# Sixteen of the 22 inner chunks of two down projections as seven block products instead of eight

## The reference, cut to what matters

```python
def _swiglu(x, w_gu, w_down):
    gate, up = jnp.split(x @ w_gu, 2, axis=-1)
    return (jax.nn.silu(gate) * up) @ w_down
...
h = _layernorm(ALPHA * x + 0.5 * _swiglu(x, p['ffa_w_gu'], p['ffa_w_down']), p['ln1_g'], p['ln1_b'])
...
y = _layernorm(ALPHA * h + 0.5 * _swiglu(h, p['ffb_w_gu'], p['ffb_w_down']), p['ln3_g'], p['ln3_b'])
```

## Time and profile before

| | |
|---|---|
| median of three runs | 1212.16 us (1209.61 to 1213.62) |
| span of the profiled execution | 1212.0 us |
| TensorE busy | 1180.2 us in 12282 matmuls |
| VectorE busy | 819.3 us |
| ScalarE busy | 512.3 us |
| GpSimd busy | 90.4 us |
| FFN a | from about 8 to 373 us of the span |
| FFN b | from about 861 us to the end |

### The profile page before, as it was taken

One profiled execution on the slowest core, in us unless ns is written; L12 is line 12 of the kernel. 1 busy time (PEld: TensorE's weight loads), 2 busy tenths in 40 slices (PEclk: granted clock), 3 DMA queues, 4 the chain that ended last, 5 costly groups with the idle time before them and its releaser, 6 DMA issues.

```text
span 1212.0 us, 29018 instructions
## 1 busy us (share of the span) xinstructions
PE 1180.2 (97%) x12282; PEld 1064.8 (88%) x12282; DVE 819.3 (68%) x1155; ACT 512.3 (42%) x794; POOL 90.4 (7%) x89
## 2 busy tenths in 40 slices
PE   9999999999999999999989999999999999999996
PEld 8999999999998988886556445798999999999995
DVE  5875795699557653454665653787885797579754
ACT  5432442244233864443543434334642343244323
POOL 0000000000020210001450111020000000000021
PEclk9999999999999999999999999999999999999998
DMA  6223223233313667647765998642223232323211
GB/s 222 96 90 135 87 100 110 93 106 106 101 51 117 254 242 235 235 157 223 234 221 168 315 319 277 223 176 71 86 81 111 94 105 89 135 76 107 97 36 71
DMA packets 56723, 177.35 MB, mean 146 GB/s; under 512 B 7186, under 2 KB 7443, under 8 KB 47251
## 3 DMA queue, kind: packets, MB, share of 16 engines
q1 hardware_dynamic: 53426, 169.48, 40.9%
q10 hardware_dynamic: 3168, 6.02, 1.5%
HBM read 164.64 MB, written 10.83 MB: 145 GB/s over the span
## 4 chain that ended last, share of the span: by engine, by line
PE 90%; DVE 5%; ACT 2%; issue 1%; DMA 1%; SPq 0%; DVEq 0%
PE banks L388 37%; PE banks L593 30%; PE banks L1296 3%; PE banks L2106 2%; PE banks L2036 2%; PE banks L411 2%; PE banks L1043 2%; PE banks L2288 1%; PE banks L2334 1%; PE banks L1589 1%; PE banks L2184 1%; PE banks L908 1%; PE banks L2409 1%; DVE weights_lo L367 1%; PE banks L2278 1%
## 5 line engine op out<-in xcount | busy, mean ns | idle before, releaser
L367 DVE TENSOR_TENSOR weights_lo<-weights_raw,weights_hi 128x1024 fp32r<-128x1024 f32 (+1 forms) x90 | 106.8, 1196 | 98.3 <-ACT weights_hi L359 97.7
L359 ACT ACTIVATE weights_hi<-weights_raw 128x1024 fp32r<-128x1024 f32 (+1 forms) x90 | 90.8, 1018 | 164.5 <-PE banks L388 142.8
L388 PE MATMUL banks<-hidden_hi,weights_hi 128*128 128x260 f32 x576 | 116.3, 283 | 0.0
L388 PE MATMUL banks<-hidden_hi,weights_lo 128*128 128x260 f32 x576 | 115.5, 282 | 0.0
L388 PE MATMUL banks<-hidden_lo,weights_hi 128*128 128x260 f32 x576 | 115.5, 282 | 0.0
L388 PE MATMUL banks<-x_hi,weights_hi 128*128 128x260 f32 x544 | 111.2, 285 | 0.1
L388 PE MATMUL banks<-x_hi,weights_lo 128*128 128x260 f32 x544 | 109.5, 283 | 0.0
L388 PE MATMUL banks<-x_lo,weights_hi 128*128 128x260 f32 x544 | 109.3, 283 | 0.0
L388 PEld LDWEIGHTS banks<-x_hi,weights_hi 128*128 128x128 f32 x544 | 83.7, 188 | 12.7 <-issue 11.7
L593 PE MATMUL banks<-x_sums_hi,more_weights_hi 128*128 128x260 f32 x320 | 90.6, 283 | 0.0
L593 PE MATMUL banks<-x_sums_hi,more_weights_lo 128*128 128x260 f32 x320 | 90.5, 283 | 0.0
(11 more groups left out here) (409 smaller groups left out, 3008.3 us busy)
## 6 DMA issues: line engine op xcount, KB each, us to landing
cache_pages<-in_cache_k SPq DMA_DIRECT2D x128, 256.0 KB, 3.7
weights_raw<-in_gate_up_b SPq DMA_DIRECT2D x22, 1024.0 KB, 4.7
weights_raw<-in_gate_up_a SPq DMA_DIRECT2D x21, 1024.0 KB, 4.8
cache_pages<-in_cache_v SPq DMA_DIRECT2D x56, 256.0 KB, 3.9
weights_raw<-in_w_in SPq DMA_DIRECT2D x13, 1024.0 KB, 5.4
projected<-in_cache_v SPq DMA_DIRECT2D x48, 256.0 KB, 3.7
weights_raw<-in_down_a SPq DMA_DIRECT2D x8, 896.0 KB, 4.6
weights_raw<-in_down_b SPq DMA_DIRECT2D x8, 896.0 KB, 4.6
```

The costliest lines, as they stand in the source:

```text
L359: nc.scalar.activation(WH[pr.slot(i, k)][:, 0:nk, :], RAW[slot][:, 0:nk, P * (k % 2):P * (k % 2) + P], ACT.Copy).then_inc(split_hi, 1)
L367: nc.vector.tensor_tensor(WL[pr.slot(i, k)][:, 0:nk, :], RAW[slot][:, 0:nk, P * (k % 2):P * (k % 2) + P], WH[pr.slot(i, k)][:, 0:nk, :].bi ...
L388: mm = nc.tensor.matmul(acc[s][:, a, 0:HALF], w[slot][:, t, :], x[:, k0 + t, HALF * a:HALF * a + HALF], start=begins and t == tiles[0] and ...
```

## The change

**What it does.** The groups become 8, 8 and 6 chunks. For the first two groups the down product is no longer made of slabs. It is made of pairs like the up product: one pair is two output chunks, over the group's 8 hidden chunks and both halves of tokens, in seven block products (84 matmuls in place of 96). There are four such pairs per group, eight per feed-forward part. The third group of 6 keeps its slabs. So a feed-forward part has 26 pairs in a row (4 up, 4 down, 8 up, 4 down, 6 up) and then the slabs.

For that the hidden chunks of the first two groups need sums too: for chunk `t` and chunk `t+4` of a group, three sums and one more difference of 260 elements. `hidden_sum_pool` makes the first of them on GpSimd when chunk `t` is there, `hidden_sums_pool` the other three on GpSimd when chunk `t+4` is there; for the last chunk of a group VectorE makes them (`hidden_sums_vector`). They are split into high and low parts by `hidden_sums_high` and `hidden_sums_low` (780 and 260 elements each).

Of the four sums of weights of each pair, three move from VectorE to GpSimd (`outer_sums_pool`: one instruction of 2 x 512 elements, `second_sum_pool`: 512), and the fourth (`whole_sum_vector`) stays on VectorE. The sums now lie in the tile in which their low parts are written. So GpSimd may only begin the sums of pair `j+1` when all products of pair `j-1` are done (`weights_room`), and `sums_low` waits for the fourth sum too. `raw_room` waits for that sum as well. A down pair ends in `added_vector`, two additions of 520 elements to `Y` on VectorE, where an up pair ends in `hidden_vector` and `hidden_low`.

The first down pair of a group begins before the last chunk is there: `first_down_pair_tensor` takes tiles 0 and 1 of all seven products, then tile 2, then tile 3 in another order (`LATE_ORDER`), and waits between them for the low parts. The host lays out `w_down` in the new order; bytes moved stay the same.

```diff
-GROUPS = (7, 7, 8)
-GROUP_AT = (0, 7, 14)
+GROUPS = (8, 8, 6)
+GROUP_AT = (0, 8, 16)
...
+    LATE_ORDER = (1, 2, 3, 6, 7, 5, 4)
...
-        def outer_sums_vector(dve, sv, j):
-
-            dve.wait_ge(raw_ready[sv.raw_slot(j)], sv.raw_count(j))
+        def outer_sums_pool(pool, sv, j):
+
+            pool.wait_ge(raw_ready[sv.raw_slot(j)], sv.raw_count(j))
+            weights_room(pool, sv, j)
+            wait_from_one(pool, g("summed"), 3 * sv.pair(j))
             raw, to = raw_quarters(sv, j), sums_of(sv, j)
-            two = to[:, :, :].rearrange("p (a b) n -> p a b n", b=2)[:, :, 0, :]
-            nc.vector.tensor_tensor(two, raw[:, 0:2, :], raw[:, 3:4, :].broadcast_to([P, 2, 4 * P]), ALU.add).then_inc(g("summed"), 1)
-            dve.wait_ge(g("summed"), 3 * sv.pair(j) + 1)
-            nc.vector.tensor_tensor(to[:, 1, :], to[:, 0, :], raw[:, 1, :], ALU.add).then_inc(g("summed"), 1)
+            two = to.rearrange("p (a b) n -> p a b n", b=2)[:, :, 0, :]
+            pool.tensor_tensor(two, raw[:, 0:2, :], raw[:, 3:4, :].broadcast_to([P, 2, 4 * P]), ALU.add).then_inc(g("summed"), 1)
+
+        def second_sum_pool(pool, sv, j):
+            raw, to = raw_quarters(sv, j), sums_of(sv, j)
+            pool.wait_ge(g("summed"), 3 * sv.pair(j) + 1)
+            pool.tensor_tensor(to[:, 1, :], to[:, 0, :], raw[:, 1, :], ALU.add).then_inc(g("summed"), 1)
...
+            dve.wait_ge(g("summed"), 3 * sv.pair(j) + 3)
...
+        def hidden_operands(which, t):
+            if which == 7:
+                return [s[:, t, HALF:TOK] for s in (HH, HL)]
+            if which in X_SUM:
+                return [s[t][:, (5, 6, 4).index(which), :] for s in (HSH, HSL)]
+            h, c = (1 if which == 3 else 0), (t if which == 1 else 4 + t)
+            return [s[:, c, HALF * h:HALF * h + HALF] for s in (HH, HL)]
...
+        def first_down_pair_tensor(pe, sv, j):
+
+            q = sv.outputs[j][0]
+            pe.wait_ge(h_ready, sv.all_chunk(GROUP_AT[q] + 6) + 1)
+            for which in sv.ORDER:
+                pe.wait_ge(g("parts_lo"), part_done(sv, j, PART_OF[which]))
+                bank_drained(pe, sv, j, which)
+                if which in X_SUM:
+                    pe.wait_ge(g("h_sums_lo"), sv.sums_of(q, 1))
+                product_tensor(pe, sv, j, which, hidden_operands, range(2))
+            pe.wait_ge(g("h_sums_lo"), sv.sums_of(q, 2))
+            for which in sv.ORDER:
+                product_tensor(pe, sv, j, which, hidden_operands, (2,))
+            for which in sv.LATE_ORDER:
+                if which == 2:
+                    pe.wait_ge(h_ready, sv.all_chunk(GROUP_AT[q] + 7) + 1)
+                if which == 6:
+                    pe.wait_ge(g("h_sums_lo"), sv.sums_of(q, 3))
+                product_tensor(pe, sv, j, which, hidden_operands, (3,)).then_inc(g("product"), 1)
...
+        def added_vector(dve, sv, j):
+
+            q, i = sv.outputs[j]
+            dve.wait_ge(g("combined"), combined_at(sv, j, "gates"))
+            for n, (parts, by) in enumerate(((scratch(j, FIRST, 2), ALU.add), (scratch(j, THIRD, 2, 3), ALU.subtract))):
+                y = halves(Y[:, 2 * i + n, :])
+                if q:
+                    ins = nc.vector.tensor_tensor(y, y, parts, by)
+                else:
+                    ins = nc.vector.scalar_tensor_tensor(out=y, in0=y, scalar=2 * ALPHA, in1=parts, op0=ALU.mult, op1=by)
+            ins.then_inc(g("combined"), 1)
...
+        def hidden_sums_pool(pool, sv, j):
+
+            c, t = sv.chunk(j), sv.ups[j][1] - 4
+            sums, other = HSW[t], HL_WHOLE[:, t, HALF:TOK]
+            pool.wait_ge(g("combined"), combined_at(sv, j, "hidden"))
+            pool.tensor_tensor(sums[:, 1, :], sums[:, 0, :], scratch(j, END), ALU.add).then_inc(g("h_sums"), 1)
+            pool.tensor_tensor(other, scratch(j, END), other, ALU.subtract).then_inc(g("h_sums"), 1)
+            pool.wait_ge(g("h_sums"), sv.sums_count(c, 0))
+            pool.tensor_tensor(sums[:, 2, :], sums[:, 1, :], scratch(j, FIRST), ALU.subtract).then_inc(g("h_sums"), 1)
...
+        def hidden_sums_low(dve, sv, j):
+            q, slot = sv.ups[j]
+            t = slot - 4
+            dve.wait_ge(g("h_sums_hi"), sv.sums_of(q, t))
+            nc.vector.tensor_tensor(HSL[t], HSW[t], HSH[t].bitcast(f32), ALU.subtract)
+            nc.vector.tensor_tensor(HL[:, t, HALF:TOK], HL_WHOLE[:, t, HALF:TOK], HH[:, t, HALF:TOK].bitcast(f32),
+                                    ALU.subtract).then_inc(g("h_sums_lo"), 1)
...
+        def first_down_pair_vector(dve, sv, j):
+
+            gates_vector(dve, sv, j - 1)
+            hidden_sums_low(dve, sv, j - 2)
+            hidden_vector(dve, sv, j - 1)
+            hidden_sums_vector(dve, sv, j - 1)
+            hidden_low(dve, sv, j - 1)
+            outer_low(dve, sv, j + 1)
+            whole_sum_vector(dve, sv, j + 1)
+            hidden_sums_low(dve, sv, j - 1)
+            sums_low(dve, sv, j + 1, "first")
+            second_vector(dve, sv, j)
+            third_vector(dve, sv, j)
+            ends_vector(dve, sv, j)
+            sums_low(dve, sv, j + 1, "last")
...
+            for j in range(sv.pairs - 1):
+                outer_sums_pool(pool, sv, j + 1)
+                second_sum_pool(pool, sv, j + 1)
+                if summed_hidden(sv, j - 1):
+                    slot = sv.ups[j - 1][1]
+                    if slot < 4:
+                        hidden_sum_pool(pool, sv, j - 1)
+                    elif slot < 7:
+                        hidden_sums_pool(pool, sv, j - 1)
```

475 lines of the change are left out of this document (270 added, 205 removed).

## The result

The kernel with the change takes **1246.41 us** (median of 4 runs, 1242.39 to 1247.68) against 1210.95 us (4 runs, 1209.61 to 1213.62): ratio 1.0287 with an interval of 1.0265 to 1.0309. It is slower by 35 us. The sign was forecast and the time lies in the range; the size was put at 21 us. The profiled execution took 1242.39 us, its span is 1240.6 us, 28.6 more than that of before.

What follows compares the result with a forecast made beforehand. TensorE was taken to set the time, with VectorE close behind in the pairs. 1212.0 less 22.2 for fewer matmuls plus 43.0 for late VectorE and GpSimd steps gave 1232.8, predicted 1233 us, range 1203 to 1262.

Steps and rivals of the forecast that it cites:

- TensorE's part: Feed-forward products: fewer matmuls save 11.1 us a part, 22.2 us for both, giving 1190 if TensorE never waited more.
- rival 2: Pairs: GpSimd's sums cost VectorE nothing, so the kernel takes 1190 to 1193 us; chance 0.06.
- VectorE's step alone: VectorE's own work per pair without GpSimd: 7.98 us in a light step, 11.46 in a first down pair, against 10.08.
- The length of a turn: Time a GpSimd sum holds up VectorE's two-SBUF-operand work: 2.2 us for 2 x 512 elements, 1.1 for 512, 0.56 for 260.
- Rival 3: Pairs: VectorE is held for GpSimd's whole instruction, 29 us more for both parts, 1262 us; chance 0.16.
- The step table: 25 steps of a feed-forward part, VectorE and GpSimd together: 10.3 to 12.95 us each against 10.08, over by 19.6 us.
- The 2.5 of hand-offs: Pairs: a VectorE that is waited for pays about 0.1 us a step in hand-offs, 2.5 us a part.
- the 2.1 us of GpSimd's time that I let be free: Steps with three short sums: 2.1 us of GpSimd's time delays nothing, covered by VectorE's reads of banks.
- The slack: Pairs: a VectorE step may end late without delaying TensorE, so 2.8 us is taken off once per part.
- What I costed at nothing: Loads, ScalarE, the norm beside the third group's shorter slabs, and TensorE's clock staying at 1.00: no cost.
- Rival 1: Light steps take 9.1 us and pay back the heavy steps' debt, so the kernel ends faster, 1207 us; chance 0.15.
- Rival 4: The change doesn't do what it says, in TensorE's matmul count or VectorE's sums; given no chance.

Runs made afterwards that it cites:

- e8: The changed kernel with GpSimd's sums of weights and hidden chunks in the pairs replaced by writes of zeros, waits kept: 1192.78 us, ratio 0.9857 to the kernel before.
- e1: The changed kernel with GpSimd's three weight sums replaced by writes of zeros, same places and waits: 1198.38 us, ratio 0.9904 to the kernel before.

## Why the prediction was right, and where its size was wrong

**TensorE's part.** As forecast: 12090 matmuls, and e8, in which no turn is left, takes 1192.8 us (rival 2's time, 1190 to 1193). In FFN a the change is worth 96 x 0.12 = 11.5 us.

**What was lost.** The first x-product of the mixing part starts at 370.06 before and at 384.54 after: 14.5 us, so 26.0 us went into waits or slowness in FFN a; 21.5 were forecast. They are: 17.0 us in the 14 waits for low parts of weights; 3.6 more at these waits, since around each of them two matmuls start 0.16 and 0.10 us later than 0.12 and the wait explain; 3.0 in two stretches at half clock; 1.2 us in front of the mean (L1098, below); 0.3 for the last hidden chunk; and some 0.9 that I can't name.

**VectorE's step alone.** Right. With L655 at 1217 ns in e8, VectorE is busy for 7.9 to 8.2 us of a light step (forecast 7.98) and idle for the rest, and an e8 step is 10.06 us but for the first down pair.

**The length of a turn.** Right for 512 elements (1.1), nearly for 1024. VectorE in the step of the first down pair:

```profile
114.63 3.05 DVE L655 TENSOR_TENSOR weights_lo<-weights_lo_whole,weights_hi 128x1024 fp32r<-128x1024 f32 x1
```

and GpSimd there:

```profile
114.13 2.46 POOL L630 TENSOR_TENSOR more_weights_lo_whole<-weights_raw 128x1024 f32<-128x1024 f32 x1 [9.50 <-PE banks L689]
```

L655 takes 1.22 alone, so it began in truth at 114.63 + 3.05 - 1.22 = 116.46, that is 2.33 us after GpSimd's start (forecast 2.2) and 0.13 before GpSimd's instruction ended. For 512 elements it was 1.12 of 1.27: in both the turn ends 0.13 to 0.15 before the instruction. So a step's weight sums hold 3.45 us and not 3.3. The Trainium skill (SBUF — State Buffer, section Who interferes with whom) calls the ports that both engines share an exclusive lock; by that rule the turn would be the whole instruction. The trace comes near it, 0.13 to 0.15 us short. Rival 3 put 0.5 us more into each step; the trace has 0.15. The same section says that GpSimd contends by its reads and not by writes alone; e1 and e8 agree (1229 and 1217 ns beside memsets).

**The step table.** The sum is nearly right, its parts are not. The steps add up to 274.8 us where 272.0 were forecast, and 2.5 more as hand-offs: a difference of 0.3. That it is so small is luck: an error of 7.4 us in the heavy steps and one of 7.1 in the light ones cancel. Heavy steps (1 to 4, 13 to 16) took 51.75 each four for 48.05, 7.4 us more, and the others 171.3 for 175.9, 4.6 less. The 2.5 of hand-offs don't show in them either: the 17 light steps take 10.08 us on average, just a pair. (Four of the 14 waits, 3.3 us, still stand at the ends of light steps, of 8, 11, 20 and 23, the ones of 12.4 to 12.5 us.) **The step that failed is the 2.1 us of GpSimd's time that I let be free in a step with three short sums.** In step 1 nothing was free: it lost 5.2 us to turns where GpSimd's work of a step is 4.98, because the next pair's sum began inside it. In steps 2, 3, 14 and 15 the forecast held (12.1): in step 14, from 211.78 to 223.99, VectorE loses 3.0 of 4.98. The first down pair (steps 4 and 16) was put 1.2 us too low. I took GpSimd's sums as one set per step. They follow TensorE's products (`weights_room`), so in a step that runs late two of them fall into one and none into the one after the next: hence 13.2 and 14.2 next to 8.1, in a kernel whose forecast had no step under 10.3.

**The slack.** Wrong by some 1.7 us a part: I took 2.8 off and added 2.0 for two late chunks at the ends. In place of 0.8 gained, 0.9 were lost. The first `gates_vector` came at 65.85, where e8, without turns, has it at 64.99, so VectorE began late; and in the last five steps, 49.0 us for 50.4, it caught up, so that at the end nothing was owed (VectorE is idle for 1.89 us before it):

```profile
340.66 0.97 DVE L788 TENSOR_TENSOR scratch<-banks,scratch 128x780 f32<-128x780 f32 x1 [1.89 <-PE banks L689]
```

The same event is at 316.41 before and at 316.63 in e8. So 24.25 us are lost up to there: 0.2 without any turn, 0.9 by the late start, and 23.2 in steps that take 274.8 us and not e8's 251.6.

**What I costed at nothing.** Loads and ScalarE: right, no wait names them in the pairs. The norm beside shorter slabs: wrong by 1.2 us a part. TensorE waits 1.2 us in front of the mean (L1098) in after, e1 and e8 alike and not in before, so it is no turn's. The trace names nothing that it waits for there; that the shorter slabs of the third group leave it too little time is my reading. TensorE's clock: **wrong**. It stayed at 1.00 where the earlier trace rows had it, but not in the pairs. Two stretches of after (us, busy and count of PE, PEld, DVE, ACT, POOL, granted clock, DMA):

```profile
103.85:107.26 3.41, 3.41 (x18) 3.41 (x17) 3.31 (x7) 1.28 (x2) 0.78 (x1) 0.50 0.00 0
236.97:240.38 3.41, 3.41 (x18) 3.41 (x17) 3.31 (x8) 1.27 (x2) 0.39 (x1) 0.50 0.00 0
```

At 0.50, the lower of its two levels, matmuls start 0.22 us apart and not 0.12: 16 start in the 3.41 us (the 18 count two that began earlier), where 28 would. That is 1.5 us lost each time. Both come behind TensorE's waits of 0.7 to 2.3 us in steps 1 to 3 and 13 to 15. FFN b has two as well, from 947 and from 1081 us. Before, and in e8, the pairs of both parts have none.

**The rivals.** Rival 1, debt paid back (1207): the light steps did fall to 8.1 at times, but 5 to 8 took 10.35 on average and not 9.1, since the sum that was missing in one fell into another (12.5). Rival 2, no cost (1190): only with the reads gone. Rival 3 (1262): above; of the 0.5 us a step that it adds the trace has a third. Rival 4: no.

**The sum.** Its terms as printed give 21.3 and not 21.5, and the nine terms of "8.0 us into the step" give 8.2; neither changes the reading. With 96 fewer matmuls at 0.12 the gain is 11.5 us a part, not 11.1.

**The rest to 35 us.** The median of after lies 4 us above the profiled run, and no trace shows it. The mean granted clock of its four runs is 0.985 to 0.988 and does not put them in the order of their times, so the cause stays open.

**Not tried.** GpSimd's 512 sum placed wholly under `gates_vector`'s read; down pairs in one group only; what activity of TensorE brings the half clock.
